# Decoder step with paged latent attention: cached latents loaded twice, rotary keys in strips, a maximum by groups, three bank pairs for pages

## The reference, cut to what matters

```
for page in the 16 pages of a sequence:          # page_table gives its number
    ckv = cache_ckv[page]                        # 128 x 256 latents
    kp  = cache_kpe[page]                        # 128 x 32 rotary keys, shared by the 8 heads
    kn, v = split(ckv @ w_mla_kvb)               # per head: 64 key and 64 value columns
    kn = rms_norm(kn, g_k_nope)
    s  = (qn . kn + qp . kp) * scale             # 8 heads x 8 queries
    online softmax over all pages and the 8 new tokens; o += p . v
```

## Time and profile before

| | |
|---|---|
| median of 3 runs | 1220.82 us (1220.02 to 1220.86) |
| the profiled execution | 1220.83 us, span 1219.0 us, granted clock 0.986 |
| PE busy | 1177.4 us (97%) |
| DVE, ACT, POOL busy | 609.9, 367.9, 297.1 us |
| page stage, first to last page matmul | 309.5 to 608.4 us |
| a sequence in steady state | 38.4 us |

### The profile page before, as it was taken

The page is one execution under the profiler, slowest core; times in us unless marked ns, Lnnn a source line. Parts: engine busy times, 40 slices in busy tenths (PEclk is TensorE's granted clock), DMA queues, the critical chain, the costliest instruction groups (busy, mean ns, idle before and its releaser), DMA issues.

```text
span 1219.0 us, 22441 instructions
## 1 busy us (share of the span) xinstructions
PE 1177.4 (97%) x8096; PEld 1048.0 (86%) x8096; DVE 609.9 (50%) x1030; ACT 367.9 (30%) x847; POOL 297.1 (24%) x180
## 2 busy tenths in 40 slices
PE   7999999899999999999989998999999999999997
PEld 4799896566999989999867774799999999999997
DVE  0659554767466566665622135543454344434442
ACT  4222034455454444544401025333320003321000
POOL 0126041810465655656511110200000000000000
PEclk9999999999999999999989998999999999999999
DMA  8432102120152212222007221132222222222102
GB/s 336 156 104 71 55 2 61 35 66 14 43 183 75 76 41 54 67 75 71 5 1 293 70 62 60 52 105 87 86 69 87 86 81 75 87 86 85 55 0 77
DMA packets 61604, 97.42 MB, mean 80 GB/s; under 512 B 22961, under 2 KB 41554, under 8 KB 61458
## 3 DMA queue, kind: packets, MB, share of 16 engines
q1 hardware_dynamic: 60946, 94.56, 24.8%
q0 software_dynamic: 576, 1.84, 0.4%
HBM read 91.12 MB, written 5.25 MB: 79 GB/s over the span
## 4 chain that ended last, share of the span: by engine, by line
PE 81%; DVE 7%; POOL 4%; issue 3%; ACT 2%; DMA 1%; POOLq 0%; DVEq 0%; SPq 0%; ACTq 0%
PE bank L1341 34%; PE bank L718 8%; PE bank L780 4%; PE bank L798 4%; PE bank L1152 3%; PE bank L1154 3%; POOL stat L2611 3%; PE bank L1153 3%; PE bank L742 2%; PE bank L1104 2%; PE bank L1180 2%; PE bank L1042 2%; PE bank L1084 1%; PE bank L960 1%; DVE stat L2189 1%
## 5 line engine op out<-in xcount | busy, mean ns | idle before, releaser
L1341 PE MATMUL bank<-hr,wr 128*128 128x288 f32 x1536 | 205.2, 296 | 1.0 <-DVEq L2297 1.0
L1341 PEld LDWEIGHTS bank<-hr,wr 128*128 128x128 f32 x1536 | 204.9, 189 | 1.4 <-issue 1.4
L1341 PE MATMUL bank<-ur,wr 128*128 128x288 f32 x1536 | 205.3, 296 | 0.0
L1341 PEld LDWEIGHTS bank<-ur,wr 128*128 128x128 f32 x1536 | 205.0, 189 | 0.1
L2611 POOL TENSOR_TENSOR stat<-stat,cst 128x32 f32<-128x32 f32 x32 | 173.7, 5428 | 2.5
L1152 PE MATMUL bank<-wq_high,c_parts 128*128 128x288 f32 x512 | 162.2, 317 | 3.5 <-ACT hT L1653 2.5
L1154 PE MATMUL bank<-wq_low,c_parts 128*128 128x288 f32 x512 | 151.5, 296 | 0.0
L1153 PE MATMUL bank<-wq_high,c_parts 128*128 128x288 f32 x512 | 150.6, 294 | 0.0
L2401 DVE CAST wr<-ring 128x1024 fp32r<-128x1024 f32 x64 | 44.4, 694 | 208.6 <-PE bank L1341 207.9
L2189 DVE TENSOR_REDUCE stat<-hT 128x8 f32<-128x512 f32 x128 | 86.9, 684 | 78.5 <-ACT hT L1653 74.0
L1152 PEld LDWEIGHTS bank<-wq_high,c_parts 128*128 128x128 f32 x512 | 96.5, 188 | 8.2 <-ACT hT L1653 3.9
(11 more groups left out here) (392 smaller groups left out, 1833.3 us busy)
## 6 DMA issues: line engine op xcount, KB each, us to landing
ring<-in_ring_w_dram SPq DMA_DIRECT2D x106, 512.0 KB, 3.6
arena<-in_cache_ckv_dram SPq DMA_DIRECT2D x128, 128.0 KB, 2.0
arena<-in_mk_t_dram SPq DMA_DIRECT2D x8, 512.0 KB, 4.0
arena<-in_cache_mv_dram SPq DMA_DIRECT2D x8, 512.0 KB, 10.4
mixT<-in_x_dram SPq DMA_DIRECT2D x1, 2048.0 KB, 12.7
arena<-in_cache_kpe_dram SPq DMA_DIRECT2D x128, 16.0 KB, 1.7
out_dram<-hT SPq DMA_DIRECT2D x4, 512.0 KB, 3.2
mixT<-in_w_qb_dram SPq DMA_DIRECT2D x1, 1152.0 KB, 5.8
```

Source lines behind the costliest of these rows:

```text
L1341: ins = mm(outs[c][:, 0:HALF], w[:, ew, k, :], src[:, ex, k0 + k, c * HALF:(c + 1) * HALF], start=(start and k == 0 and n == 0), stop=(sto ...
```

## The change

Four edits:

1. The host passes the cached latents a second time with latent columns in the partitions (`ckv_t`), and the rows with the rotary keys ahead of the latents (`page_rows`, 288 columns). `transposed_pages` is gone; `high_parts` and `turned` read the loaded tiles `pages_t` (four slots of a pair) in SBUF. SP's `load_pair` reads two page numbers and issues four DMAs, two of turned latents and two of rows; pair n + 4 waits until DVE has read pair n's slot.
2. Rotary keys are turned eight pages at a time, at pages 6 and 14: 8 matmuls against the identity, each with the 32 key columns of a page as stationary operand, into 32 partitions of bank 7 each. ACT copies 256 columns. The rotary matmuls and their copies stand at pages 6, 7, 14 and 15.
3. The maximum over the scores is taken group by group: after each group of four pages but the first one elementwise maximum of 256 columns, and at the end one reduction over 256 columns and a 64-column step for the new tokens. The last group and these steps stand at pair 2, behind the low part of pair 3.
4. Pages go round three bank pairs (0 and 1, 2 and 3, 4 and 5; page 15 takes the second), and three buffers of squares.

```diff
+            def load_pair(b, par, n, read=None, summed=None):
+                page = [page_number(b, 2 * n + e) for e in range(2)]
+                for e in range(2):
+                    if read is not None and e == 0:
+                        sp.wait_ge(S("c_low"), read)
+                    sp.dma_start(pages_t[n % 4][:, e, :, :]..., ckv_t[page[e]]...)
+                for e in range(2):
+                    if summed is not None and e == 0:
+                        sp.wait_ge(S("pv_out"), summed)
+                    sp.dma_start(cpg[par][:, 2 * n + e, 0:ROPE + KR], page_rows[page[e]]...)
+            def stream(b, par, first=False, last=False):
+                for n in range(4):
+                    load_pair(b, par, n + 4, b * 8 + (n + 1))
+                if not last:
+                    for n in range(4):
+                        load_pair(b + 1, 1 - par, n, b * 8 + (n + 5), None if first or n else b)
             sp.wait_ge(S("turned"), 4)
-            load_latents(0, 0)
-            load_keys(0, 0)
+            load_pair(0, 0, 0)
             sp.wait_ge(S("phase_end"), MET[3])
-            load_keys(1, 1)
-            load_latents(1, 1)
+            for n in range(1, 4):
+                load_pair(0, 0, n)
+            stream(0, 0, first=True)
...
 (PE)
-                    if n < 7:
-                        transposed_pages(par, n + 1, tb)
                     pe.wait_ge(S("c_low"), b * 8 + (n + 1))
                     for e in range(2):
                         j = 2 * n + e
-                        if not (first and j < 2):
-                            pe.wait_ge(S("kr_free"), b * NPG + (j - 1))
+                        if j % 8 == 6:
+                            o = reopen(pe, "kpt_first") if first and j < 8 else reopen(pe, ("kpt", j // 8), b, 5)
+                            for v in range(2):
+                                for q in range(4):
+                                    ins = mm(o[32 * q:32 * q + 32, v * P:(v + 1) * P],
+                                             cpg[par][:, j - 6 + 4 * v + q, 0:ROPE], ident, start=True, stop=True)
+                            filled(ins, ("kpt", 0))
+                        if not (first and j < 3):
+                            pe.wait_ge(S("kr_free"), b * NPG + last_page_there(j) + 1)
...
-                            if j == 5:
+                            if j == 6:
                                 softmax_max(prev)
...
 (ACT, in sequence; high_parts now copies pages_t[n % 4])
-                rope_keys(b, first)
...
+                    if j % 8 == 6:
+                        rope_keys(b, j // 8)
                     page_out(b, j, par)
...
 (DVE, in group_scores)
+                if g:
...
+                    below = sc[par][:, 0:4, :].rearrange("p j c -> p (j c)") if g == 1 else top
+                    V.tensor_tensor(top, below, s4, ALU.max).then_inc(S("tops"), 1)
...
+            def all_scores_max(b, par):
+                V.tensor_reduce(mx[:, 0:64], tops.rearrange("p j c -> p c j"), AX.X, ALU.max)...
+                V.tensor_tensor(top, top, sc[par][0:NS, NPG, :], ALU.max).then_inc(S("mx"), 1)
...
 (DVE, in sequence)
+                    if not first and n == 2:
+                        group_scores(b - 1, 3, 1 - par)
+                        all_scores_max(b - 1, 1 - par)
...
                     page_sums(b, 2 * n)
-                    if not first and n == 1:
-                        group_scores(b - 1, 3, 1 - par)
+                    if not first and n == 0:
                         new_scores(b - 1, 1 - par)
+                    if n == 7 and not last:
+                        turned(b + 1, 0)
```

More of the change, by code:

```diff
@@ L501, in beside, with closing, third, last_page_there @@
             return w[:, :, :, at_q:at_q + QH]
+        def closing(name, b):
+            return name + "_end" if isinstance(b, int) and b == NB - 1 else name
+        def third(j):
+            return 1 if j == NPG - 1 else j % 3
+        def last_page_there(j):
+            return j - 2 if j in (1, NPG - 1) else j - 4 if j == 0 else j - 3
         def page_columns(b_par):
@@ L624, in page_number @@
                 where = page_sb[0:1, bass.ds(b * NPG + j, 1)]
-                return sp.value_load(where, min_val=0, max_val=cache_ckv.shape[1] - 1)
-            def load_keys(b, par, anew=False):
-                for j in range(NPG):
-                    page = page_number(b, j)
-                    if anew and j == 0:
-                        sp.wait_ge(S("kpT"), b - 1)
-                    sp.dma_start(kpg[par][:, j * ROPE:(j + 1) * ROPE], cache_kpe[0, bass.ds(page, 1), :, :].rearrange(
-                        "a p c -> p (a c)")).then_inc(S(f"page_k{par}"), 16)
@@ L636, in load_latents @@
-            def load_latents(b, par, anew=False):
-                for j in range(NPG):
-                    page = page_number(b, j)
-                    if anew and j == 0:
-                        sp.wait_ge(S("pv_out"), b - 1)
-                    sp.dma_start(cpg[par][:, j, 0:KR], cache_ckv[0, bass.ds(page, 1), :, :].rearrange(
-                        "a p c -> p (a c)")).then_inc(S(f"page_c{par}_{j // 4}"), 16)
+                return sp.value_load(where, min_val=0, max_val=ckv_t.shape[0] - 1)
@@ L652, in _ @@
             with sp.Fori(0, (NB - 2) // 2) as i:
-                for par in range(2):
-                    b = i * 2 + (2 + par)
-                    load_keys(b, par, anew=True)
-                    load_latents(b, par, anew=True)
+                stream(i * 2 + 1, 1)
+                stream(i * 2 + 2, 0)
+            stream(NB - 1, 1, last=True)
             sp.wait_ge(S("phase_end"), MET[4])
@@ L1122, in new_tokens, with sequence @@
                           start=True, stop=True), "scn")
[L1124 to L1127 removed]
+            def sequence(b, par, first=False):
                 prev = None if first else b - 1
[L1129 to L1130 removed]
                 if prev is not None:
                     new_tokens(prev)
[L1133 to L1137 removed]
                 pe.wait_ge(S("wq"), b * 2 + 4)
@@ L1155, in sequence @@
                                          start=False, stop=(k == KC - 1))
-                            if j % 4 == 0:
-                                if j == 0 and f == 0:
-                                    pe.wait_ge(S("kpT"), b + 1)
-                                ins = mm(o[:, WQ - QH:WQ - QH + P], kpT[:, j // 4, :],
+                        if j % 8 >= 6:
+                            if j % 8 == 6:
+                                pe.wait_ge(S("kpT"), b * 2 + (j // 8 + 1))
+                            for f in range(2):
+                                ins = mm(bank[2 * third(j) + f][:, WQ - QH:WQ - QH + P], kpT[:, j % 2, :],
                                          qpd[:, bass.ds(b, 1), 2 * f:2 * f + 2, :].rearrange("p a q c -> p (a q c)"),
@@ L1198, in _ @@
             half_output(3)
-            weighted_T(NB - 1, "_last")
+            weighted_T(NB - 1)
             pe.wait_ge(S("pcT"), NB)
@@ L2240, in take_sums, with divide @@
                 dve.nop().then_inc(S("pv_out"), 1)
-            def divide(b, last=""):
-                o = full(dve, "pct" + last, b, 4)
+            def divide(b):
+                o = full(dve, closing("pct", b), b, 5)
                 V.reciprocal(rl, o[:, 128:192]).then_inc(S("pv_r"), 1)
@@ L2272, in sequence @@
                         divide(b - 1)
-                    if n == 7 and not last:
-                        turned(b + 1, 0)
                     page_sums(b, 2 * n + 1)
@@ L2711, in memory_layout, with turned_pages @@
     return np.ascontiguousarray(c.reshape(NB, 2, P, XH, XD).transpose(0, 4, 1, 3, 2).reshape(NB, XD, -1))
+def turned_pages(c):
+    n, rows, width = c.shape
+    return np.ascontiguousarray(c.reshape(n, rows, width // P, P).transpose(0, 3, 2, 1).reshape(n, P, -1))
 def key_layout(w):
```

160 lines of the change are left out of this document (75 added, 85 removed).

## The result

The changed kernel takes 1208.61 us (median of 4 runs, 1205.21 to 1210.36), the kernel before, measured beside it, 1220.84: a ratio of 0.9896, 95% interval [0.9869, 0.9923], so 12 us or 1% faster. The forecast was 1200, with a range from 1192 to 1210. The profiled execution is the fastest of the four, 1205.21 us, span 1203.4.

A forecast was written before the change was run, and what follows sets the result against it. TensorE was taken as the bound, busy 37.83 of 38.4 us a sequence. Savings and additions summed to -21.2 us against 1220.83, giving 1199.6, said as 1200 us, with a range from 1192 to 1210.

The forecast's parts named there:

- Latents' transposes: TensorE, page stage: removing 62 groups of four transposes at 0.445 us each saves 27.6 us.
- Narrow matmuls: TensorE, turning rotary keys: 0.47 us of matmuls plus the change of width, 0.75 us a group, sixteen groups add 12.0 us.
- Bank 7: TensorE at page 14: waits 0.36 us for DVE's division to free the bank, 7 times, adding 2.5 us.
- Weighted sum: TensorE, waiting for the exponential: the 0.16 us idle stays and 0.1 us a sequence is added, 0.7 us.
- The tie of 5.3 and 5.25 us: Before the weighted sum: DVE and ACT need some 5.3 us, TensorE has 5.25 us of work in front.
- Stall before page 6: TensorE, seven sequences: low part now ahead of DVE's maximum, so the stall goes, 7 x 0.42 = 2.9 us saved.
- DMA and SP, "Hidden": Page loads: 3.2 us issue a pair and 2.1 landing stay covered; cover gone if landing took 9 us.
- Rival 3: Page loads through four slots: pages come late and the kernel is slower, 1262 us at a 17 us landing; chance 0.04.
- The start: First sequence: first page matmul 1.0 us earlier, then a stall of 1.8 us waiting for pair 1.
- The end: Last sequence's chain without pages: the transposed maximum starts 1.2 us earlier.
- The clock's 2.4 us: End of the stage: with half the idle time the clock stays at 2.4 GHz, 2.4 us saved; bounds 0 and 2.4.
- rival 1: Page stage: the ACT, DVE and POOL chain ends last, costing 1 to 2 us a sequence, 1207 to 1214; chance 0.15.

The follow-up runs named there:

- narrow_twice: ring_late with the eight narrow matmuls of each group of rotary keys issued twice; 1204.84 us, ratio to the kernel before 0.9871.
- divide_early: Changed kernel with DVE's division ahead of the page sums of page 12 instead of behind them; 1205.57 us, ratio to the kernel before 0.9888.
- ring_late: Changed kernel with the 8 tiles of output weights issued behind the last sequence's pages instead of the first's; 1197.22 us, ratio to the kernel before 0.9829.
- whole_max: Changed kernel with one maximum reduction over all 17 blocks at pair 2 instead of group by group; 1208.55 us, ratio to the kernel before 0.9912.
- before_ring_late: Kernel before, with the 8 tiles of output weights issued behind the last sequence's pages, as control; 1220.38 us, ratio to the kernel before 1.0011.
- late_and_early: Changed kernel with the edits of ring_late and divide_early together, nothing else; 1194.94 us, ratio to the kernel before 0.9803.
- two_pairs: ring_late with pages going round two bank pairs and two buffers of squares instead of three; 1198.82 us, ratio to the kernel before 0.9828.
- rows_first: ring_late with the rows of pairs 1 to 3 of the first sequence issued ahead of the meeting; 1196.85 us, ratio to the kernel before 0.9816.
- pairs_and_max: ring_late with both edits of two_pairs and whole_max; 1199.43 us, ratio to the kernel before 0.9832.

## Why the prediction was right, and where it was not

- **Latents' transposes.** Pages with a group of them in front were 2.04 us apart and are 1.59: 0.45 a group, as forecast.
- **Narrow matmuls.** 0.77 us a group where 0.75 was forecast, and narrow_twice splits it nearly as the forecast did, 0.44 for the matmuls and 0.33 for going there and back, of which 0.08 is not the width's. The Trainium skill, TensorEngine Tiling (Array Packing), section Key Properties, says that a change of the tiling mode drains TensorE. The 0.25 us that is left agrees with such a cost; that it is a drain no run here shows.
- **Bank 7.** 0.39 us where 0.36 was worked out, with the releaser named; divide_early takes 0.30 of it away.
- **Weighted sum.** Forecast as 0.1 us worse, it is 0.3 better (page 10 to 11: 6.17 before, of which 0.16 was the idle time in the earlier trace rows, 5.87 now). The tie of 5.3 and 5.25 us went the good way in all seven sequences of this profile. It is a tie all the same: in ring_late and in five of its variants two to four of the seven sequences have 6.04 to 6.16 us there. This is 0.4 of the 0.5 us by which a steady sequence beats the forecast; I put the last 0.1 down to the rotary products, which now stand four together behind a page and no longer two and two inside it, with one slower start fewer. That was not tried.
- **Stall before page 6.** It is gone, as said. The reason given, that the maximum went elsewhere, is half shown: putting it elsewhere in the kernel before only moved the stall, and the form of the maximum didn't matter.
- **DMA and SP, "Hidden".** This is the step that failed. The steady state holds: SP takes 3.2 to 3.4 us a pair and TensorE waits for no page. But the cover was worked out without what else stands in SP's queue. Eight tile issues put pair 4 off by 4.4 us (341.05 to 345.40), and 4 MB in front of it turned a landing of about 2.2 us into 7.30. The sentence that the cover would be gone at a landing of 9 us left out the first of the two; together they are 11.7 us. Rival 3 named the 4 MB as contention in its sum and then priced only the steady state. It came true in one sequence of the seven behind the first: 9.5 us in the trace, 8.2 by the ratios.
- **The start.** The first matmul came 0.87 us earlier for 1.0 forecast. The stall of 1.8 us came as two pieces, 1.43 us of page 0 at half speed and 0.61 before page 2, in sum 2.0. The first sequence lost another 0.6 us at page 6, where pair 4, issued at TensorE's own pace and so without slack, was late, and 1.2 us before its page 14. No DMA is late there. The low part of pair 7 stands on DVE behind the scores of the second group of pages, and these wait for POOL's power:

```profile
324.58 5.43 POOL L2624 TENSOR_TENSOR stat<-stat,cst 128x32 f32<-128x32 f32 x1
```

```profile
330.05 0.42 DVE L2197 TENSOR_TENSOR arena<-arena,stat 128x256 f32<-128x256 f32 x1 [1.74 <-POOL stat L2624]
...
331.08 0.43 DVE L2208 TENSOR_TENSOR hT<-arena 128x256 f32<-128x256 f32 x1
...
332.02 0.68 DVE L2179 TENSOR_TENSOR c_parts<-arena,c_parts 128x512 fp32r<-128x512 f32 x1
```

```profile
332.75 0.64 PE L1138 MATMUL bank<-cst,arena 128*32 128x128 f32 x16 [1.16 <-DVE c_parts L2179]
```

  The sum had no term for this. In a steady sequence the trace has no such wait; there the delayed weighted sum of 3.69 us stands on TensorE between pages 10 and 11, and the first sequence has none. That this is what gives the chain its time elsewhere was not tried. All variants with the new pages have the wait, whole_max with 0.84 us of idle time, since it has no group maximum (L2208) in the way.
- **The end.** The idle time before the transposed maximum is 1.4 us shorter (2.29 before, 0.90 now) for 1.2 forecast. But 0.44 of it is taken by the rotary matmuls, which now stand behind the last page, and 0.27 by a longer wait ahead of the output matmuls (0.46 us for 0.19): between two executions at full clock there, before_ring_late and late_and_early, the way from the last page matmul to the last weighted sum is 16.96 and 16.29 us, 0.67 shorter. The clock's 2.4 us were not the change's to give. With the same code and the same idle times there, 0.89 and 0.78 us, late_and_early has the full clock:

```profile
596.58 0.33 PE L1090 MATMUL bank<-cst,arena 128*128 128x128 f32 x1 [0.89 <-DVE arena L2228]
597.69 0.43 PE L1095 MATMUL bank<-arena,cst 64*128 64x64 f32 x2 [0.78 <-DVE arena L2235]
598.05 4.15 PE L1174 MATMUL bank<-mixT,ring 128*128 128x288 f32 x16
```

and so has before_ring_late behind an idle time of 2.29 us:

```profile
619.66 0.33 PE L1091 MATMUL bank<-cst,arena 128*128 128x128 f32 x1 [2.29 <-DVE arena L2218]
...
621.12 4.15 PE L1180 MATMUL bank<-mixT,ring 128*128 128x288 f32 x16
```

The miss adds up: 9.5 (second sequence) + 2.0 (first sequence: 0.2 more of the stall, 0.6 and 1.2) - 3.5 (0.5 us in seven sequences) is 8.0 us against the stage's 16.6 - 8.8 = 7.8.

The forecast held by luck and by a wide range. The gain is 12.2 us for 21.2; 1208.61 lies outside the 1193 to 1207 that the prediction gave its own forecast, and two of the four runs lie above 1210. It does lie in rival 1's 1207 to 1214, but that rival's mechanism, a chain that costs 1 to 2 us in every sequence, is not there: steady sequences are shorter than forecast.

## What to carry to other kernels

When a change loads just in time what was loaded far ahead, list everything that the same queue issues in the stretch, and price the first use behind each foreign block: the longer of its issue time and its bytes at the rate that the DMA engines reach. Here that is an estimate of 10.5 us (4 MB at about 400 GB/s) against 4.4 of issue, and the data came 9.6 us late (17.94 against 8.30). Look at which queue waits first for the late data, since what stands behind it on that engine, here a small copy, stops the others earlier than the data's own consumer would. Follow the first pass of a loop by itself: work of the pass before, behind which others could hide, is not there yet. Two limits in one place hide each other: an experiment that removes one of them and gains nothing doesn't show that it is free.

## What was not expected of the hardware

- The clock at one place differs between executions of the same code. From the last page matmul to the last weighted sum the changed kernel and ring_late took 17.99 and 17.98 us, two_pairs, rows_first and late_and_early 16.29, without any edit there; the kernel before took 19.67, before_ring_late 16.96. From there to the end the profiles fall at 589.7 or at 590.5 to 591.1 us. That is 2 to 4 us of chance in any comparison of two profiles, more than most terms here.
- At the start page 0 was steady: all nine profiles of the changed kernel and its variants without extra transposes have it at 2.77 to 3.02 us, and the two with them 1.67. The stretch at half speed was not: it ends after 12 to 15 products in six of the nine, and after 23 or 24 in whole_max, pairs_and_max and rows_first.
